# Two mixture-of-experts layers: rows made by GpSimd in token order, tile norms in a new order, routing and dispatch in fewer operations

## The reference, cut to what matters

```python
x = x + o @ w_out;  x = x + (silu(n(x) @ w_gate) * (n(x) @ w_up)) @ w_down     # block 1
for i in range(2):                                    # block 2: one even and one odd layer
    mod = (silu(c) @ mod_w[i] + mod_b[i]) split in 6  # gates, shifts and scales, for tokens and context
    x = x + mod[2] * (mixer(modulate(x, ...)) @ w_out)
    tok = rms_norm(x, g) * (1 + mod[4]) + mod[3]      # 768 rows in layer 0, 512 in layer 1
    # group of 4 by softmax and argmax, then the best 2 of its 4 experts, weights normalised
    x = x + mod[5] * sum over the 2 chosen of 16 experts of (silu(tok @ wg) * (tok @ wu) * weight) @ wd
```

## Time and profile before

| | |
|---|---|
| times of 3 runs | 2084.7, 2090.4, 2091.33 us; median 2090.4 us |
| profiled execution | 2086.35 us, of which its span is 2084.6 us |
| busy: PE, DVE, ACT, POOL | 1939.7, 1106.0, 654.2, 191.1 us |
| granted TensorE clock, mean | 0.974 of full speed |
| moved by DMA | 313.88 MB, mean 151 GB/s |

### The profile page before, as it was taken

One profiled execution on the slowest core, in us unless ns is written; L12 is line 12 of the kernel. 1 busy time (PEld: TensorE's weight loads), 2 busy tenths in 40 slices (PEclk: granted clock), 3 DMA queues, 4 the chain that ended last, 5 costly groups with the idle time before them and its releaser, 6 DMA issues. The chain is left out here.

```text
span 2084.6 us, 28875 instructions
## 1 busy us (share of the span) xinstructions
PE 1939.7 (93%) x10968; PEld 1062.2 (51%) x10968; DVE 1106.0 (53%) x1878; ACT 654.2 (31%) x1294; POOL 191.1 (9%) x214
## 2 busy tenths in 40 slices
PE   7999999999999999899998999799988999988993
PEld 4554874444444444455645764543325678645330
DVE  2001771387787200367754642567756667446773
ACT  2002661100000100242313641356652656333550
POOL 3000110011111000011200000011102000001101
PEclk9999999999999999999999999999999999999996
DMA  8633101476776320410110000689947020048995
GB/s 262 154 81 131 42 12 41 161 245 240 260 247 223 140 81 20 139 41 11 71 41 29 33 22 0 270 318 346 365 180 265 1 82 2 1 155 330 384 406 191
DMA packets 104247, 313.88 MB, mean 151 GB/s; under 512 B 8695, under 2 KB 42647, under 8 KB 85680
## 3 DMA queue, kind: packets, MB, share of 16 engines
q1 hardware_dynamic: 75008, 184.79, 24.8%
q0 software_dynamic: 22448, 103.09, 13.9%
q10 hardware_dynamic: 6656, 24.15, 2.9%
HBM read 281.52 MB, written 35.73 MB: 152 GB/s over the span
## 5 line engine op out<-in xcount | busy, mean ns | idle before, releaser
L2958 PE MATMUL ps<-wide 128*128 128x512 f32 x704 | 306.0, 594 | 2.3 <-issue 1.3
L2958 PEld LDWEIGHTS ps<-wide 128*128 128x128 f32 x704 | 132.4, 190 | 171.8 <-issue 170.6
L2416 PE MATMUL ps<-wide,X 128*32 x448 | 197.5, 594 | 2.1 <-DVE X L2568 2.1
L2416 PE MATMUL ps<-Z,X 128*32 128x512 f32 x1344 | 197.9, 594 | 0.0
L1667 PE MATMUL ps<-wide 128*128 128x512 f32 (+1 forms) x384 | 150.0, 548 | 0.5 <-issue 0.5
L1178 DVE SCALAR_TENSOR_TENSOR Z<-Z,wide 128x2048 f32<-128x2048 f32 x56 | 131.6, 2350 | 2.8
L824 PE MATMUL ps<-T 64*128 64x256 f32 (+1 forms) x888 | 110.0, 378 | 8.7 <-DVE nm L963 6.7
L1417 PE MATMUL ps<-wide 128*128 128x512 f32 x256 | 112.1, 595 | 2.1 <-issue 1.0
L3283 DVE TENSOR_TENSOR X<-ps,X 128x512 f32<-128x512 f32 x16 | 11.1, 692 | 191.4 <-PE ps L328 98.5
L389 ACT ACTIVATE T<-ps 128x512 f32<-128x512 f32 (+2 forms) x139 | 70.8, 537 | 130.6 <-PE ps L1417 109.8
L2432 PE MATMUL ps<-T,gw 128*32 x336 | 104.0, 608 | 8.1 <-ACT X L2489 8.1
(11 more groups left out here) (394 smaller groups left out, 3363.6 us busy)
## 6 DMA issues: line engine op xcount, KB each, us to landing
wide<-in_experts SPq DMA_DIRECT2D x64, 1024.0 KB, 8.5
Z<-in_mod_w POOLq DMA_DIRECT2D x32, 1024.0 KB, 5.2
T<-in_experts SPq DMA_DIRECT2D x32, 1024.0 KB, 10.9
X<-in_mod_w POOLq DMA_DIRECT2D x16, 1024.0 KB, 5.4
moe_out<-X ACTq DMA_DIRECT2D x28, 512.0 KB, 8.5
wide<-in_w_gate SPq DMA_DIRECT2D x22, 512.0 KB, 5.3
wide<-in_w_up SPq DMA_DIRECT2D x22, 512.0 KB, 6.7
wide<-in_w_in SPq DMA_DIRECT2D x10, 1024.0 KB, 10.2
```

The costliest lines, as they stand in the source:

```text
L2416: last = pe.matmul(ps[rows, t % 2, :], mo.xT[:, c, rows], w_rows, start=(c == 0), stop=(c == DK - 1))
L2958: last = pe.matmul(self.gu.bank(u)[:, 0:self.n], w, self.rhs(c), start=(c == 0), stop=(c == DK - 1))
```

## The change

1. `TileNorm(inside=True)`: all pairs but the last are turned and taken inside the last block (pair p behind tile 2p+2), and DVE scales tile i right after it took tile i. `RowAndTileNorm` likewise: behind tile 1 the context pair, behind tile 2 the first pair, and both norms of a tile at once.
2. In the first block's w_out, PE does the first half (256 of 512 token columns) of two of the FFN's first units in the gap around the last pair (`between`, `after`); the FFN then does their other halves. The FFN's PSUM banks are turned by 4.
3. `RowStores` (new) runs in the stage of each mixer's projection. POOL loads the shift and scale rows and the gain, broadcast over the partitions, and the router's constants. DVE makes gain*(1+scale) once for each set. Then POOL, for each tile once it is scaled, spills X, multiplies the row by the gain, adds the shift and stores the row. `ModSums` stores all four parts of the modulation rows for it (16 small DMAs instead of 8).
4. `Router`: no turning back of HT, no copies or stores on ACT, no single spill. The logits of all pairs but the last are made in the projection's gap (`between`). The constants that dispatch needs are set at its start. Group and expert choice take fewer operations.
5. `Dispatch`: one scan over experts and tiles instead of sums tile by tile, rounding by adding and subtracting a large constant instead of comparing and counting. The lists are made in four column groups with the row table moving, turned once, and summed by DVE. The row list comes ahead of the experts' list, and POOL starts the first two gathers inside this stage.

```diff
@@ Linear
         if self.norm:
             self.last_block(pe, u0)
+            if self.between:
+                self.between(pe, self.norm)
             self.norm.tensor(pe)
+            if self.after:
+                self.after(pe)
@@ last_block
-            if i == len(self.tiles) - 2 and len(self.norm.pairs) == 3:
-                self.norm.turn(pe, 0)
+            for p in self.norm.behind.get(i, ()):
+                self.norm.turn(pe, p)
@@ _take
-                    if self.norm and c0 == self.blocks[-1][0] and i:
-                        self.norm.tile(eng, ch, i - 1)
-                        if i == len(self.tiles) - 1 and len(self.norm.pairs) == 3:
-                            self.norm.take(eng, name, 0)
+                    if self.norm and c0 == self.blocks[-1][0]:
+                        self.norm.tile(eng, ch, i)
+                        for p in self.norm.behind.get(i, ()):
+                            self.norm.take(eng, name, p)
@@ TileNorm
+        self.behind = {2 * p + 2: [p] for p in range(len(self.pairs) - 1)} if inside else {}
+        self.rest = range(len(self.pairs) - 1 if inside else 0, len(self.pairs))
@@ RowAndTileNorm
+        self.behind, self.pairs = {1: [0], 2: [1]}, self.norm.pairs
@@ ModSums
     def stores(self, i):
-        return {1: (0, 1), 2: (2, 3)}.get(i % 3, ())
+        return (0, 1, 2, 3) if i % 3 else ()
@@ RowStores (new)
+    def gpsimd(self, pool, ch):
+        k, mo = self.k, self.k.mo
+        for dst, src in self.loads:
+            pool.dma_start(dst, src).then_inc(k.row_mods_landed.sem, 16)
+        for dst, src in ((mo.iota, k.C["iota"]), (mo.token, k.C["token"]), (mo.before, k.C["before"]), (mo.pace, k.C["pace"][:, self.l, :])):
+            pool.dma_start(dst, src).then_inc(k.small_landed.sem, 16)
+        pool.wait_ge(k.row_gains_ready.sem, self.ready + len(self.sets))
+        for i, t in enumerate(self.norm.tiles):
+            gain, shift = self.sets[0 if t < ST else 1]
+            row = self.place(i)
+            pool.wait_ge(k.norm_rows.sem, self.norm.rows + i + 1)
+            pool.dma_start(self.away[:, t, :], k.X[:, t, :]).then_inc(k.spilled.sem, 16)
+            ch.step(pool.tensor_tensor(row, self.norm.hn[:, t, :], gain, ALU.mult))
+            ch.wait()
+            ch.step(pool.tensor_tensor(row, row, shift, ALU.add))
+            ch.wait()
+            pool.dma_start(self.rows_out[t * P:(t + 1) * P, :], row).then_inc(k.rows_stored.sem, 16)
+
+    def vector(self, dve, ch):
+        k = self.k
+        dve.wait_ge(k.row_mods_landed.sem, self.landed + 16 * len(self.loads))
+        for gain, _ in self.sets:
+            dve.scalar_tensor_tensor(gain, gain, 1.0, self.gain, ALU.add, ALU.mult).then_inc(k.row_gains_ready.sem, 1)
@@ Router
-        self.lots = [(a, min(a + ST, len(tiles))) for a in range(0, len(tiles), ST)]
+        self.lots = [(0, len(tiles) - 2), (len(tiles) - 2, len(tiles))]
@@ Router.gpsimd
-        for dst, src in loads:
-            pool.dma_start(dst, src).then_inc(k.small_landed.sem, 16)
-        pool.dma_start(*self.spill).then_inc(k.spilled.sem, 16)
-        pool.wait_ge(k.spilled.sem, self.spilled + 16)
+        self.stores.await_consts(pool)
+        self.stores.await_spilled(pool)
         for dst, src in self.rows_gate:
             pool.dma_start(dst, src).then_inc(k.small_landed.sem, 16)
-        pool.wait_ge(k.small_landed.sem, self.consts + 64 + 16 * len(self.rows_gate))
+        self.stores.await_rows(pool)
@@ Router.tensor
-        for v in range(2 * len(self.tiles)):
-            t, hf = self.tiles[v // 2], v % 2
-            self.rows.may_fill(pe, v)
-            for c in range(4):
-                last = pe.transpose(self.rows.bank(v)[:, c * P:(c + 1) * P],
-                                    k.HT[:, 4 * hf + c, t * P:(t + 1) * P], k.ident[:, :])
-            self.rows.filled(last)
         pe.drain().then_inc(k.places_free.sem, 1)
@@ Dispatch.tensor
-        keep_awake(pe, k, 3, 36)
+        keep_awake(pe, k, 7, 36)
         pe.wait_ge(k.step_done.sem, self.hot + 2)
         for u in range(2 * n):
-            last = pe.matmul(self.banks.bank(2)[:, 0:2 * self.m], mo.row_hot[:, u, :], mo.quad_hot[:, u, 0:2 * self.m],
-                             start=(u == 0), stop=(u == 2 * n - 1))
+            j = u % 4
+            last = pe.matmul(self.banks.bank(2)[32 * j:32 * j + 32, 0:P], mo.quad_hot[:, u, :], mo.row_hot[:, u, :],
+                             start=(u < 4), stop=(u >= 2 * n - 4))
         self.banks.filled(last)
+        self.banks.taken(pe, 2)
+        self.banks.filled(pe.transpose(self.banks.bank(3)[:, 0:P], mo.listed, k.ident[:, :]))
+
+    def gpsimd(self, pool, ch):
+        pool.wait_ge(self.k.tokens_ready.sem, self.tokens + 1)
+        self.gathers(pool)
@@ Dispatch.vector, its end
+        self.banks.await_full(dve, 2)
+        self.banks.take(2, dve.tensor_copy(mo.listed, self.banks.bank(2)[:, 0:P]))
+        self.banks.await_full(dve, 3)
+        parts = self.banks.bank(3)[:, 0:P].rearrange("p (j c) -> p c j", j=4)
+        self.banks.take(3, dve.tensor_reduce(k.row_pair[:, :], parts, AXX, ALU.add))
+        self.banks.taken(dve, 3)
+        dve.tensor_copy(k.row_token[:, 0:m], k.row_pair[:, 0:m]).then_inc(k.tokens_ready.sem, 1)
...
         dve.drain().then_inc(k.lists_ready.sem, 1)
-        self.banks.await_full(dve, 2)
-        dve.tensor_copy(k.row_weight[:, 0:m], self.banks.bank(2)[:, m:2 * m])
-        self.banks.take(2, dve.tensor_copy(k.row_token[:, 0:m], self.banks.bank(2)[:, 0:m]))
@@ GatedTurned
+    def begin(self, pe, u, norm=None):
+        if norm:
+            norm.pair_taken(pe, 0)
+        for s in self.slots[0]:
+            self.k.rg.await_landed(pe, s)
+        self.unit(pe, u, slice(0, self.n // 2))
+        self.begun.add(u)
@@ two_blocks
+        projection.early.then.between = lambda pe, norm: feed.begin(pe, 0, norm)
+        projection.early.then.after = lambda pe: feed.begin(pe, 1)
...
-        add(Together(k, Loading(k, gate_loads(0, 2, 2)), even.then))
+        add(Together(k, Loading(k, gate_loads(0, 2, 2)), row_stores(0, even.then, 2), even.then))
```

More of the change, by code:

```diff
@@ L55 @@
 LAG = 2
+ROUND = float(3 << 22)
 SLOT = 2048
@@ L486, in scalar @@
         for i in range(len(self.tiles)):
-            if i == len(self.tiles) - 1 and len(self.pairs) == 3:
-                self.take(act, "act", 0)
             self.square(act, i)
-        for p in range(len(self.pairs) == 3, len(self.pairs)):
+            for p in self.behind.get(i, ()):
+                self.take(act, "act", p)
+        for p in self.rest:
             self.take(act, "act", p)
@@ L2215, in vector @@
-        self.banks.take(1, dve.tensor_tensor(mo.count, total[:, n - 1, :], before[:, n - 1, :], ALU.add))
-        self.banks.taken(dve, 1)
-        do(dve.tensor_scalar(mo.count, mo.count, 1.0 / QUARTER, None, ALU.mult))
-        count_of(mo.quarters, mo.count, NEXP, 4 * n - 1, ALU.is_gt)
-        do(dve.tensor_scalar(mo.quarters, mo.quarters, 1.0, None, ALU.add))
+        size = NEXP * n
+        self.banks.await_full(dve, 0)
+        self.banks.take(0, dve.tensor_tensor_scan(mo.sums[:, 1:size + 1], mo.joined[:, 0:size], self.banks.bank(0)[:, 0:size],
+                                                  0.0, ALU.mult, ALU.add))
@@ L2945, in __init__, with unit @@
         self.chunks = 2 * len(blocks)
-        self.gu = Banks(k, ["act", "dve"] * self.chunks, 0, 6)
+        self.gu = Banks(k, ["act", "dve"] * self.chunks, 0, 6, turn=4)
+        self.begun = set()
+    def unit(self, pe, u, columns):
+        k, s, half, which = self.k, self.slots[u // 4], u // 2 % 2, u % 2
+        for c in range(DK):
+            w = k.rg.slot(s[c // 4]).rearrange("p (c a n) -> p c a n", c=4, a=2)[:, c % 4, which, half * P:(half + 1) * P]
+            last = pe.matmul(self.gu.bank(u)[:, columns], w, self.rhs(c)[:, columns], start=(c == 0), stop=(c == DK - 1))
+        return last
+    def begin(self, pe, u, norm=None):
[5 more added lines that the diff above has]
+        self.begun.add(u)
     def tensor(self, pe):
@@ L2955, in tensor @@
             self.gu.may_fill(pe, u)
-            for c in range(DK):
-                w = k.rg.slot(s[c // 4]).rearrange("p (c a n) -> p c a n", c=4, a=2)[:, c % 4, which, half * P:(half + 1) * P]
-                last = pe.matmul(self.gu.bank(u)[:, 0:self.n], w, self.rhs(c), start=(c == 0), stop=(c == DK - 1))
-            self.gu.filled(last)
+            self.gu.filled(self.unit(pe, u, slice(self.n // 2 if u in self.begun else 0, self.n)))
             if u % 4 == 3:
@@ L3338, in moe @@
             add(experts)
+            dispatch.gathers = experts.first_gathers
             experts.w.late_from = first[1]
```

309 lines of the change are left out of this document (172 added, 137 removed).

## The result

The changed kernel takes 2115.32 us (median of 4 runs, 2113.86 to 2119.82); the kernel before, run beside it, 2088.68 us. The ratio is 1.0127, with a 95% interval of 1.0111 to 1.0143: 26.6 us slower, where 2089.4 was predicted in a range that ended at 2098. The profiled execution has a span of 2112.8 us, 28.2 more than before. All times in this document are of executions in the chip's usual, fast state; of e6's four executions one took 5006.86 us and is left out.

What follows compares the result with a forecast made beforehand. PE was taken as busy almost throughout, so only its waits and dummy matmuls could yield time. w_out -2.8, w_down -3.5, layer 0 +2.4 and layer 1 +2.9 gave -1.0 from the 2090.4 median: 2089.4 us, range 2079 to 2098.

Steps and rivals of the forecast that it cites:

- store issue 0.54, meet 0.3: Projections' ends: last terms of POOL's 6.9 us for the last tile, with 0.3 us for the meet after issuing the store.
- POOL's two gather issues ... and 0.3: Layer 1's dispatch end: POOL's gather issues, 0.3+1.0+0.3+2.43 us, then 0.3, bound the stage's last part.
- Row stores and spills, the last issued at the stage's start, have 20 us to land: Routing and dispatch: POOL's transfers from the projection were to land within the following stage, with 20 us for it.
- w_out, -2.8: End of w_out: half units of the FFN fill PE's gap around the last pair's turn, gaining 2.8 us.
- w_down, -3.5: End of w_down: two pairs turned inside, so the next stage starts at L+12.3 instead of L+15.8, gaining 3.5 us.
- L: The moment the last tile's DVE take starts, which is where the last matmul ended; other times count from it.
- The projections' ends, +3.9 and +4.6: Routing starts at L+14.0 because POOL must finish the last tile: 3.9 us later in layer 0, 4.6 in layer 1.
- The first collision: Projections' ends: DVE's residual addition collides with POOL's operation, making the last tile 0 to 2.4 us late; 1.2 taken.
- Rival C: Slower: in the projections, DVE's scaling also collides with POOL's second operation, 4.7 us per layer: 2098.8 us, chance 0.22.
- Routing and dispatch, 27.9 and 26.4 us: Stage lengths in layer 0 and layer 1 from the stage's start, 1.5 and 1.7 us shorter than before.
- B: Faster: PE's clock recovers for dispatch's dummies, no last-tile collision, lists at their lower bound: 2081.6 us, chance 0.31.
- D: Layer 1's experts: down matrices start earlier, so PE's late weight waits vanish, 3 us more gain; chance 0.02.

Runs made afterwards that it cites:

- e6: Changed kernel without POOL's product and sum, so rows are stored without gain and shift, all drains kept: 2108.5 us, ratio 1.0100 to the kernel before.
- e4: Changed kernel with the last tile's copy and row store issued by ACT instead of POOL, all drains kept: 2099.0 us, ratio 1.0048 to the kernel before.
- e5: Changed kernel with the experts' first weight loads held back until the row stores have landed, all drains kept: 2102.8 us, ratio 1.0067 to the kernel before.
- e1: Changed kernel with a small memset instead of POOL's drain at four meets (projections' and dispatches' ends): 2088.0 us, ratio 0.9994 to the kernel before.
- e9: e1 plus 22 dummy products on PE in w_down, before the last turn: 2080.6 us, ratio 0.9958 to the kernel before.
- e8: e1 plus POOL's last row moved into the routing and dummy products in w_down and both layers' projections: 2079.9 us, ratio 0.9955 to the kernel before.
- e2: Changed kernel with a memset instead of POOL's drain only at the two meets ending the projections: 2097.7 us, ratio 1.0042 to the kernel before.
- e10: e8 with the dispatch's dummy products cut from 36 to 27 (layer 0) and 18 (layer 1): 2073.4 us, ratio 0.9923 to the kernel before.
- e11: e10 with the experts' dummy products cut from 17 to 10 (layer 0) and 30 to 13 (layer 1): 2071.5 us, ratio 0.9920 to the kernel before.

## Why the prediction was wrong

**The step that failed.** "store issue 0.54, meet 0.3" at the projections' end and "POOL's two gather issues ... and 0.3" at the dispatch's, with "Row stores and spills, the last issued at the stage's start, have 20 us to land" behind both: these terms were too small. I took a meet to cost POOL 0.3 us whatever it had issued. Its drain waits for its DMAs to land, and in layer 0 the meet follows the last landing by 1.0 or 1.1 us in the kernel after, in e4, e5 and e6 (0.7 in layer 1 of the kernel after). From the profile of after that is 9.2 us at layer 0's projection (issue done 1329.31, PE 1338.56), 9.6 at layer 1's, 3.3 and 4.3 at the dispatches (from DVE's end): 26.4 us. e1 gives it without the trace: 2115.3 - 2088.0 = 27.3. The transfers that were to be hidden were all hidden in e1; in the kernel after they were given back at the meet. The rows of before that I used had no DMA of POOL's still in flight at a meet without a wait written for it: at the earlier trace rows POOL had issued the gate row at 1887.25 and PE was released by POOL's queue at 1891.75, but there the stage's own wait for that load explains it. The Trainium skill (PSUM — Partial Sum Buffer, "Engine vs sequencer instructions") says that a drain waits for the engine to go fully idle, and advises putting the increment on the producing instruction itself. What "idle" takes in is what the runs add: POOL's drain waited for POOL's DMAs (e1 to e6), ACT's did not wait for ACT's (e4).

**w_out, -2.8.** Right, in this trace. The FFN starts with two half units done and the first block's next stage at 704.17 instead of 706.97.

**w_down, -3.5.** The mechanism was right and its net size wrong. L there is 857.5, a turn before the last take at 859.40; the next stage starts at L+13.1 (12.3 predicted, 15.8 before); 1.0 us of the miss is the turn, 3.67 where I had put 2.7. But PE, which in the kernel before turned the middle pair between 864.46 and 870.06, within that wait, now stood idle for 6.37 us in one piece. In the kernel before the clock was low there as well (0.50 at 868 to 872) but back for the narrow matmuls; in the kernel after it was not, and the next stage paid 2.25 us more for them, a term that the prediction didn't have. The mixer's projection starts 2.55 us earlier than before, of which w_out's part is 2.8: nothing is left of w_down's in this execution. e9 shows the clock as the cause of the slow turn and narrow matmuls. In e4, e5 and e6, with the same code, the stage starts at L+12.7 to L+12.9 and the narrow matmuls take 2.79: there some 3 of the 3.5 us stand.

**The projections' ends, +3.9 and +4.6.** Right, in e1, where no drain stands behind them: the routing starts 11.6 and 11.8 us after the last take, so at L+13.5 and L+13.7 against L+14.0 predicted, +3.4 and +4.3. The first collision is there: the residual's addition took 1.65 us in layer 0 and 1.83 in layer 1 where it takes 0.69. Rival C's second collision did not come: the last tile's scaling took 0.75 us (the one before it 0.98, which began while POOL's sum ran). That a tensor_scalar can collide, which C supposed, e8's row of 2.42 us shows.

**Routing and dispatch, 27.9 and 26.4 us.** In e1 26.6 and 25.1, 1.3 us shorter each (layer 1's terms add up to 26.6, not to the 26.4 of the prediction). The lists start straight after the dummy matmuls, as predicted; what was too long is the way to the first reduce, 3.3 us (1328.63 to 1331.97) where I had put 4.3.

**The sum.** -2.8, 0, +3.4 - 2.8, +4.3 - 3.0: -0.9 us, where -1.0 was predicted and e1 measures 0.9994. That the sum is right for a kernel without the drain is luck: two errors cancel (3.5 and 3.4 us), and the first depends on the execution's clock. The two profiled executions alone would say +2.1 us (spans of 2086.7 and 2084.6), since from the start of layer 1's experts to the end e1 took 196.5 us and the kernel before 192.9. The kernel after and e2 to e10, whose experts have the same code, took 194.0 to 196.8; what of this belongs to the change no run shows.

**The rivals.** B and C didn't come. Neither they nor D was a wait that the meet itself adds, though the change puts POOL's DMAs ahead of four meets, and at each of them it had to be asked when POOL counts as done.

## What to carry to other kernels

A DMA that is issued by GpSimd and left to land behind the next stage is not hidden if the engine ends the stage with a drain: signal from its last instruction, or issue the transfer from another engine. Where a stage's end is shortened, look at what the engine does in the gap that is left: one idle piece of 6.4 us cost TensorE its clock, and in five of eight traces also the next stage's narrow matmuls. And dummy work that was off the path must be counted again when a dependent operation is moved behind it in the same queue (e10: 6.5 us). e11, at 2071.5 us, takes 0.8% less than the kernel before (interval 0.9894 to 0.9945).

## What the runs showed of the hardware

- GpSimd's drain waits for its own outstanding DMAs, plain and indirect; ScalarE's ended 6.4 us before its own store landed. In layer 0 the next stage began 1.0 or 1.1 us after the last store's landing (landings of 2.9, 8.8, 10.1 and 13.2 us), and 0.2 us after the last gather's (issued at 1363.88, 4.8 us).
- A store of 0.5 MB landed in 2.9 to 3.0 us before the expert loads began or with them held back, in 8.6 to 10.1 beside them, and in up to 13.2 when it was issued 4.7 us after they began (e6).
- The port collision hits small operations in full: 16 columns took 2.42 us (0.11 otherwise) and 24 columns 2.06 (0.18) beside GpSimd's 1024, and moving GpSimd's work only changed which of VectorE's operations paid.
- After 6.37 us without work the granted clock of TensorE was 0.50. Its next 16 matmuls took 3.30 to 3.68 us in eight traces of the same code, and the 32 narrow ones behind them 4.98 to 5.08 in five and 2.79 in three.
